# A feature pass by Strassen's seven products in two halves of tokens, its input sums made in the pass before

## The reference, cut to what matters

```python
xn = _rms_norm(x, norm_g[l]) * (1.0 + sc_x) + sh_x
fx_in, fx_gate, qx, kx, vx, nx_gate = _split_proj(xn @ w_in[l])     # 1024 channels -> 3072, 2048 tokens
qx = _rms_norm(_heads(qx), q_norm_g[l])
kx = _rms_norm(_heads(kx), k_norm_g[l])
f_out = _fourier(fx_in, w_four[l]) * jax.nn.silu(fx_gate)
na_out = _neighbourhood_attention(qx, kx, vx, kc, vc, rel_bias[l]) * jax.nn.silu(nx_gate)
```

## Time and profile before

| | |
|---|---|
| median of 3 runs | 3400.0 us (3398.42 to 3401.95) |
| the profiled execution | 3402.36 us, span 3400.6 us, mean granted clock 0.949 |
| TensorE, matmuls | busy 3111.9 us of the span |
| VectorE, ScalarE, GpSimd | busy 1514.0, 941.8, 795.5 us |
| second token pass | from 1845 to 2113 us of the span |
| second feature pass | from 2114 to 2693 us, its first products inside the token pass's last tile |
| next stage (Fourier) | its first matmul at 2699.78 us |

### The profile page before, as it was taken

One profiled execution on the slowest core, in us unless ns is written; L12 is line 12 of the kernel. 1 busy time (PEld: TensorE's weight loads), 2 busy tenths in 40 slices (PEclk: granted clock), 3 DMA queues, 4 the chain that ended last, 5 costly groups with the idle time before them and its releaser, 6 DMA issues. The chain is left out here.

```text
span 3400.6 us, 39668 instructions
## 1 busy us (share of the span) xinstructions
PE 3111.9 (92%) x14503; PEld 2445.2 (72%) x14503; DVE 1514.0 (45%) x2504; ACT 941.8 (28%) x1520; POOL 795.5 (23%) x842
## 2 busy tenths in 40 slices
PE   3799999999988999775998999899999898999899
PEld 2588887888876666553897877677888675666687
DVE  6643333042306666386455222476000145777633
ACT  4422212110112334342222234322011133555400
POOL 5322222111112222265342222011111041000111
PEclk7899999999998999778898999999999998999999
DMA  7534335122243341314102666323211235776475
GB/s 272 184 97 116 102 101 180 61 77 75 75 127 87 90 105 55 90 47 97 43 26 82 200 185 208 109 112 123 74 74 74 99 102 134 155 158 142 112 199 148
DMA packets 325559, 390.82 MB, mean 115 GB/s; under 512 B 93879, under 2 KB 260264, under 8 KB 310696
## 3 DMA queue, kind: packets, MB, share of 16 engines
q1 hardware_dynamic: 320692, 387.11, 39.9%
q10 hardware_dynamic: 4704, 1.59, 0.2%
HBM read 256.77 MB, written 135.79 MB: 115 GB/s over the span
## 5 line engine op out<-in xcount | busy, mean ns | idle before, releaser
L691 PE MATMUL f_psum_out<-f_x_high,f_w_high 128*128 128x512 f32 (+1 forms) x1472 | 573.5, 390 | 18.8 <-DVE f_x_low L668 8.1
L691 PE MATMUL f_psum_out<-f_x_low,f_w_high 128*128 128x512 f32 (+1 forms) x1472 | 569.0, 387 | 0.0
L691 PE MATMUL f_psum_out<-f_x_high,f_w_low 128*128 128x512 f32 (+1 forms) x1472 | 568.6, 386 | 0.0
L691 PEld LDWEIGHTS f_psum_out<-f_x_high,f_w_high 128*128 128x128 f32 x1472 | 279.1, 190 | 77.9 <-issue 15.0
L691 PEld LDWEIGHTS f_psum_out<-f_x_low,f_w_high 128*128 128x128 f32 x1472 | 278.9, 189 | 56.5 <-issue 1.7
L691 PEld LDWEIGHTS f_psum_out<-f_x_high,f_w_low 128*128 128x128 f32 x1472 | 278.9, 189 | 55.5
L1351 PE MATMUL nbr_psum_o<-nbr_probT,nbr_v 128*128 128x512 f32 (+3 forms) x576 | 235.8, 490 | 0.0
L683 POOL CAST f_w_high<-f_w 128x1024 fp32r<-128x1024 f32 x41 | 42.6, 1040 | 747.8 <-PE f_psum_out L691 550.5
L532 PE MATMUL p_psum_proj<-p_w_high,p_h_high 128*128 128x512 f32 x512 | 207.5, 405 | 7.4 <-issue 4.0
L532 PE MATMUL p_psum_proj<-p_w_low,p_h_high 128*128 128x512 f32 x512 | 202.1, 395 | 0.0
L532 PE MATMUL p_psum_proj<-p_w_high,p_h_low 128*128 128x512 f32 x512 | 202.1, 395 | 0.0
(11 more groups left out here) (541 smaller groups left out, 6134.0 us busy)
## 6 DMA issues: line engine op xcount, KB each, us to landing
f_w<-in_w_fm SPq DMA_DIRECT2D x45, 512.0 KB, 5.7
side_ada_w<-in_w_ada_rows SPq DMA_DIRECT2D x24, 512.0 KB, 5.7
scratch_qkmT<-p_qkT_out SPq DMA_DIRECT2D x32, 384.0 KB, 4.6
scratch_z1T<-f_out SPq DMA_DIRECT2D x10, 1024.0 KB, 4.8
p_z<-scratch_z1T SPq DMA_DIRECT2D x16, 640.0 KB, 6.6
p_xt<-in_x SPq DMA_DIRECT2D x16, 512.0 KB, 3.9
p_staging<-in_w_tok SPq DMA_DIRECT2D x8, 1024.0 KB, 8.0
scratch_hT<-p_h_slot SPq DMA_DIRECT2D x16, 512.0 KB, 3.3
```

What stands on the lines that cost most here:

```text
L691: last = nc.tensor.matmul(self.p_out[b][:, n * BANK + lo:n * BANK + hi], self.w_parts[b][w_part][:, k, :], self.x_parts[x_part][:, n, k, l ...
```

## The change

The feature pass is made of 2x2 block products. An item is a pair of output blocks (two blocks of 128 channels) by half of the tokens (1024), so there are 24 items. In an item the weights are quadrants A (block of channels x half of k) and the input quadrants B (half of k x even or odd tiles of tokens), and Strassen's scheme in Winograd's form makes the four results of seven products: each has 4 slices of k x 3 passes = 12 matmuls of 128x128 by 128x512, the moving operand being four runs of 128 columns. This is 24 x 7 x 12 = 2016 matmuls in place of 24 x 96 = 2304.

- The four weight sums of an item are made by GpSimd (`add_weights`), the seven high parts by ScalarE (`round_w`), the seven low parts by GpSimd (`rest_of_w`). Each pair's weights are loaded twice, once for each half.
- The four input sums (T1 to T4) are made once for each pair of tiles in the token pass (`combine`: GpSimd, VectorE for the last pair) and stored beside the three plain quadrants in the scratch tensor `x2q`; x0 to x6 are loaded from it, 7 MB for each half of the tokens. For the second half they are loaded while item 11 runs, each behind the product that read it last.
- The products go through four banks of PSUM in turn, and VectorE adds them up into the outputs (`merge`, 8 operations of 128x512 in an item). Sums and transposes use two other pairs of banks. The items' order alternates kinds (`F2_ORDER`): qk, v, qk, v, qk, in, qk, in, then four gates. An item's `norm` runs inside the next item, its reciprocal in pieces of 512. The pass is written out without loops.

```diff
+class QuadrantPass:
+    A11, A12, A22, S1, S2, S3, S4 = range(7)
+    B11, B21, B22, T1, T2, T3, T4 = range(7)
+    PRODUCTS = ((A11, B11), (S2, T2), (A12, B21), (S3, T3), (A22, T4), (S1, T1), (S4, B22))
+    N, HK, BANKS = 7, KB // 2, 4
...
+    def load_w(self, sp, n):
+        if n >= 2:
+            sp.wait_ge(self.a_ready, self.N * (n - 1))
+        sp.dma_start(self.w[n % 2][:].rearrange("p m k c -> p m (k c)"),
+                     self.w_dram[self.blocks[n]:self.blocks[n] + 2].rearrange("m p c -> p m c")).then_inc(self.w_in[n % 2], 16)
+    def load_x(self, sp, half, i):
+        if half:
+            sp.wait_ge(self.prod_ready, self.N * (half * self.per_half - 1) + i + 1)
+        sp.dma_start(self.x[i][0][:].rearrange("p t k c -> p (t k c)"),
+                     self.x_dram[self.PRODUCTS[i][1], :, half * 4 * BANK:(half + 1) * 4 * BANK]).then_inc(self.x_in[i], 16)
+    def round_x(self, act, half, i):
+        act.wait_ge(self.x_in[i], 16 * (half + 1))
+        self.nc.scalar.activation(self.x[i][1][:], self.x[i][0][:], ACT.Copy).then_inc(self.x_rounded, 1)
+    def rest_of_x(self, dve, half, i):
+        dve.wait_ge(self.x_rounded, self.N * half + i + 1)
+        self.nc.vector.tensor_tensor(self.x[i][2][:], self.x[i][0][:], self.x[i][1][:], ALU.subtract).then_inc(self.x_ready, 1)
...
+    def add_weights(self, pool, n):
+        nc, w = self.nc, self.w[n % 2]
+        a11, a12, a21, a22 = (w[:, m, k:k + self.HK] for m in range(2) for k in (0, self.HK))
+        s1, s2, s3, s4 = (self.sums[:, i] for i in range(4))
+        pool.wait_ge(self.w_in[n % 2], 16 * (n // 2 + 1))
+        pool.drain()
+        nc.gpsimd.tensor_tensor(s1, a21, a22, ALU.add)
+        nc.gpsimd.tensor_tensor(s3, a11, a21, ALU.subtract)
+        pool.drain()
+        nc.gpsimd.tensor_tensor(s2, s1, a11, ALU.subtract)
+        pool.drain()
+        nc.gpsimd.tensor_tensor(s4, a12, s2, ALU.subtract).then_inc(self.sums_ready, 1)
+    def round_w(self, act, n, i):
+        a = self.PRODUCTS[i][0]
+        if n:
+            act.wait_ge(self.prod_ready, self.N * (n - 1) + i + 1)
+        if a < self.S1:
+            act.wait_ge(self.w_in[n % 2], 16 * (n // 2 + 1))
+        else:
+            act.wait_ge(self.sums_ready, n + 1)
+        self.nc.scalar.activation(self.a_high[:, i], self.quadrant(n, a), ACT.Copy).then_inc(self.a_rounded, 1)
+    def rest_of_w(self, pool, n, i):
+        pool.wait_ge(self.a_rounded, self.N * n + i + 1)
+        self.nc.gpsimd.tensor_tensor(self.a_low[:, i], self.quadrant(n, self.PRODUCTS[i][0]), self.a_high[:, i], ALU.subtract)\
+            .then_inc(self.a_ready, 1)
...
+    def product(self, pe, n, i):
+        pe.wait_ge(self.a_ready, self.N * n + i + 1)
+        if n % self.per_half == 0:
+            pe.wait_ge(self.x_ready, self.N * (n // self.per_half) + i + 1)
+        if self.N * n + i >= self.BANKS:
+            pe.wait_ge(self.prod_free, self.N * n + i + 1 - self.BANKS)
+        a_parts, x_parts = (self.a_high, self.a_low), self.x[i][1:]
+        for k in range(self.HK):
+            for at, (w_part, x_part) in enumerate(PASSES):
+                last = self.nc.tensor.matmul(self.bank(n, i), a_parts[w_part][:, i, k, :], x_parts[x_part][:, :, k, :],
+                                             start=(k == 0 and at == 0), stop=(k == self.HK - 1 and at == len(PASSES) - 1))
+        last.then_inc(self.prod_ready, 1)
...
+    def combine(eng, ops, j):
+        b11, b21, b12, b22 = (slot[b][:, k:k + HK] for b in range(2) for k in (0, HK))
+        t1, t2, t3, t4 = (combined[:, n] for n in range(4))
+        eng.wait_ge(combined_stored, 16 * (j + 1))
+        ops.tensor_tensor(t1, b12, b11, ALU.subtract)
+        ops.tensor_tensor(t3, b22, b12, ALU.subtract)
+        eng.drain()
+        ops.tensor_tensor(t2, b22, t1, ALU.subtract)
+        eng.drain()
+        ops.tensor_tensor(t4, t2, b21, ALU.subtract)
+        eng.drain().then_inc(combined_ready, 1)
...
             def move(j, b):
-                i = 2 * j + b
+                i, of_pair = 2 * j + b, bass.ds(j * BANK, BANK)
+                quadrants = d["x2q"].rearrange("s p c -> p s c")
                 wait_apart(sp, x_filled, i + 1, taken)
-                sp.dma_start(cols_of(d["x2T"], i), slot[b][:]).then_inc(slot_stored[b], 16)
+                if b == 0:
+                    sp.dma_start(quadrants[:, 0:2, of_pair], slot[0][:].rearrange("p (s k) c -> p s (k c)", s=2))\
+                        .then_inc(slot_stored[0], 16)
+                else:
+                    sp.dma_start(quadrants[:, 2, of_pair], slot[1][:, HK:].rearrange("p k c -> p (k c)")).then_inc(slot_stored[1], 16)
+                    wait_apart(sp, combined_ready, j + 1, taken)
+                    sp.dma_start(quadrants[:, 3:7, of_pair], combined[:].rearrange("p s k c -> p s (k c)")).then_inc(combined_stored, 16)
...
+            def begin_next():
+                sp.wait_ge(w_ready, MB)
                 for b in range(2):
-                    fp.load(sp, d["w_fm2"], 0, b)
-            def begin_next():
+                    sp.wait_ge(slot_stored[b], 16 * (NT // 4 + 1))
+                sp.wait_ge(combined_stored, 16 * (NT // 4 + 1))
+                fp.load_w(sp, 0)
+                fp.load_x(sp, 0, 0)
+            def go_on():
+                sp.wait_ge(gated[1], PAIRS)
+                fp.load_w(sp, 1)
+                sp.wait_ge(mix_ready[1], PAIRS)
+                sp.wait_ge(o_ready, NT - 1)
+                fp.load_x(sp, 0, 1)
                 sp.wait_ge(slices_used, 1)
-                fp.load_input(sp, d["x2T"], 0, 2)
-                sp.wait_ge(x1_ready[1], PAIRS)
-                fp.load_input(sp, d["x2T"], 2, 3)
+                fp.load_x(sp, 0, 2)
+                fp.load_x(sp, 0, 3)
             for k in range(BUFFERS, MB):
                 sp.wait_ge(w_ready, k - BUFFERS + 1)
                 begun.load_w(sp, k)
-            tiles(sp, tile, next_weights, begin_next)
+            tiles(sp, tile, begin_next, go_on)
+            sp.wait_ge(slices_used, 2)
+            fp.load_x(sp, 0, 4)
+            fp.load_x(sp, 0, 5)
+            fp.load_x(sp, 0, 6)
             move(PAIRS - 1, 1)
...
                     low(j + 1, b)
+                if b == 0 and not first:
+                    wait_apart(pool, x_filled, 2 * j, taken)
+                    combine(pool, nc.gpsimd, j - 1)
             def begin_next():
-                for b in range(2):
-                    fp.rest_of_first_weights(nc, pool, b)
+                pool.wait_ge(gated[1], PAIRS)
+                fp.add_weights(pool, 0)
+                for i in range(fp.N):
+                    fp.rest_of_w(pool, 0, i)
             low(0, 0, slice(LOW_FIRST, MB))
             low(0, 1)
...
-            fp.rest_of_input(nc, dve, 2)
+            def begin_next():
+                fp.rest_of_x(dve, 0, 0)
+                fp.rest_of_x(dve, 0, 1)
+            tiles(dve, tile, before_last=begin_next)
+            fp.rest_of_x(dve, 0, 3)
+            dve.wait_ge(xT_ready, NT)
+            dve.wait_ge(slot_stored[1], 16 * PAIRS)
+            dve.wait_ge(combined_stored, 16 * PAIRS)
+            for k in range(KB):
+                nc.vector.tensor_scalar(slot[1][:, k, :], p_x[:, k, :], g.scale_x[:, k:k + 1], g.shift_x[:, k:k + 1], ALU.mult, ALU.add)
+            dve.drain().then_inc(x_filled, 1)
+            dve.wait_ge(x_filled, NT)
+            combine(dve, nc.vector, PAIRS - 1)
+            for i in range(4, fp.N):
+                fp.rest_of_x(dve, 0, i)
...
+F2_ORDER = (0, 4, 1, 5, 2, 6, 3, 7, 8, 9, 10, 11)
...
+            for n in range(LAST + 1):
+                if n + 2 <= LAST:
+                    fp.load_w(sp, n + 2)
+                if kind(n - 1) in ("qk", "v"):
+                    store(n - 1)
+                if n == fp.per_half - 1:
+                    for i in range(N):
+                        fp.load_x(sp, 1, i)
+                if kind(n) in ("in", "gate"):
+                    store(n)
...
+            def aside(n, b):
+                used = among(n, "qk", "v")
+                if used:
+                    pe.wait_ge(aux_free[b], used)
+                if kind(n) == "qk":
+                    pe.wait_ge(sq_ready[b], among(n, "qk") + 1)
+                    for c in range(0, HT, BANK):
+                        last = nc.tensor.matmul(p_aux[b][:, c:c + BANK], ones[:], work[b][:, c:c + BANK], start=True, stop=True)
+                    last.then_inc(sum_ready[b], 1)
+                elif kind(n) == "v":
+                    pe.wait_ge(out_ready[b], n + 1)
+                    for c in range(0, HT, P):
+                        last = nc.tensor.transpose(p_aux[b][:, c:c + P], out[n % 2][b][:, c:c + P], g.ident[:])
+                    last.then_inc(turned[b], 1)
...
+            def merge(n, i):
+                first, second = out[n % 2]
+                await_product(n, i)
+                if i == 0:
+                    await_row(n, 0)
```

(35 more changed lines are left out.)

351 lines of the change are left out of this document (196 added, 155 removed).

## The result

The changed kernel takes **3472.8 us**, median of 4 runs (3468.82 to 3473.71); the kernel before takes 3401.0 (3398.42 to 3403.39). The ratio is 1.0209, with an interval of 1.0191 to 1.0227.

The account below looks back on a forecast made before the run. TensorE was taken to bound the feature pass, a ring of loads and stores the token pass. 3402.4 + 40 (token pass) - 10 (feature pass) - 1 (last stores) = 3431, less 2.4 for the median: 3429 us, range 3386 to 3464.

Parts of the forecast that it names:

- The port, 6: Feature pass: norm operations lengthened by SBUF sharing with GpSimd, allowed 0.75 us a norm, about 6 us in all.
- The bound of 44 us: Feature pass: upper limit for that sharing, if every such operation and cast stood behind a whole GpSimd operation.
- Clock, 7: Feature pass: TensorE's clock drops behind four waits of over 6 us, 1.7 us lost each, 7 us.
- Token pass, +40: Token pass: SP's wait for combine delays odd tiles' loads, 38 us over pairs 1 to 6, plus 2 for the clock.
- The ring: Token pass: loads, gating, rounding, fill, store and next load set the period; an added wait lengthens it, 6.3 us a pair.
- TensorE's own work, 482.5: Feature pass: TensorE's matmuls, sums and transposes left after product 4 starts, without waits, 482.5 us.
- The norm's timeline, 27 and 12: Items behind qk items: VectorE's norms and merges hold TensorE, 27 us behind v items and 12 behind "in" items.
- Refill, 4: Loading x0 to x6 for the second half: low parts ahead of item 12's merge 0 make TensorE wait, 4 us.
- Entry, 31.5: From the token pass's last matmul to product 4: late loads, rounding, subtracting and barrier, 31.5 us.
- Port and refill are worse: Rival, feature pass: two-input operations wait more behind GpSimd's and the refill runs at half rate, 3464 us; chance 0.2.
- the token pass's wait is covered: Rival, token pass: SP's wait for combine ends before loads are needed, only the feature pass's gain is left, 3389 us; 0.1.
- VectorE keeps up: Rival, feature pass: norms fit, so their waits and slow clock go, 3377 us; 0.1 shared with both faster rivals together.

Follow-up runs that it names:

- run 2: Changed kernel with GpSimd's weight sums and low parts in the feature pass replaced by constant fills that read nothing: 3437.5 us.
- run 3: Changed kernel with each reciprocal of the norms replaced by a minimum with 0.001, so normalisation is left out: 3403.1 us.
- run 8: Kernel of run 7 with merge 0 copying into a spare buffer, so the wait for the row's store moves to merge 2: 3362.6 us.
- Run 5: Changed kernel with pair sums stored behind the odd tile's loads and stores, and x1 to x3 loaded ahead of pair 6's sums' store: 3435.8 us.
- Run 9: Kernel of run 8 with ScalarE's fills awaiting sums made, not stored, x4 and x5 loaded later, VectorE's last-tile work earlier: 3346.0 us.
- run 7: Changed kernel with sums' store, item order, entry and refill rearranged, plus second reciprocal, scaling and merge 6 reordered on VectorE: 3398.7 us.

## Why the prediction was right in direction and wrong in size

It said 3429, in 3386 to 3464; 3472.8 lies above. Both mechanisms, a token pass made longer by a wait in SP's queue and a feature pass held up by VectorE, came as told. The sizes did not. By its own steps, with what was measured over what was forecast: token pass 45.2 for 40; entry 40.3 for 31.5; TensorE's own work 486.0 for 482.5; waits in the pass 61.1 for 49 (27 + 12 + 6 + 4); slow clock 22.8 for 7.

- **The port, 6, and the clock behind it. This step failed most.** It allowed 0.75 us a norm; a norm grew by 1.39 in the mean, by 2.9 in the four that follow merge 5 in an "in" item. Of the waits of the pass, GpSimd's reads made 25.6 us (run 2), 21.1 without the refill's part, for 6; another 11.9 followed as slow clock, for which this step had nothing. The bound of 44 us given beside it held the 37. The Trainium skill (SBUF — State Buffer, Who interferes with whom) says that a VectorE instruction with two SBUF inputs shares a read interface with GpSimd instructions that read SBUF, that GpSimd instructions which only write don't meet it, and that casts can contend as well. The trace agrees on all three: the subtraction takes 1879 ns in the mean for 1226, and 1226 again beside fills; the cast takes 1.61 us for 0.69 in the four "in" items. The Trainium skill (SBUF — State Buffer, Who interferes with whom) also says that who issues first decides who blocks. The eight casts ahead of merge 5 fit that: the one at 2222.61 began 0.28 us ahead of a GpSimd subtraction and kept its 0.70 us, and the subtraction took 1.57 for 1.29.
- **Clock, 7.** It was 22.8 in the pass: 9.5 behind the four waits of 7.6 (1.4 to 2.9 each), 7.7 behind the four of 4.0, 2.6 behind the refill's and 3.0 behind the entry's. One wait cost 2.3 in the mean for the 1.7 taken, and the number of waits was wrong: ten, not four. By itself this is the largest difference in the sum, 15.8 us.
- **Token pass, +40.** The ring came as forecast: the pair shown grew by 6.2 us (forecast 6.3), and by the loads of y 39.1 us of the 45.2 lie between the fourth and the last of them, in six long steps (forecast 38). Another 2.3 lie ahead of these and 3.8 behind the last load of y, for 2 forecast. TensorE's six waits for y are 5.6 to 7.8 us. So the step was a few us too small, and the earlier start by 5.1, which is luck, hid that in the total.
- **TensorE's own work, 482.5.** 569.9 - 61.1 - 22.8 = 486.0 after, 483.6 in run 3, 486.2 in run 8. The matmuls of the products start 0.227 us apart in the median, as those of the kernel before: a product with four runs of 128 columns costs what one of 512 costs.
- **The norm's timeline, 27 and 12.** With GpSimd's reads gone (run 2) the waits were 6.2 at the transposes, for 6.8 forecast, and 1.2 + 0.8 behind "in" items, for 3.1. This base was 6.5 us too high in all and hid part of what the port's step lacked.
- **Refill, 4.** It was a wait of 7.4, and 10 with its slow clock: merge 0 stood behind four low parts, which took 12.42 us and not 9.2, again beside GpSimd (4.5 of the 7.4 went with GpSimd's reads, and are in the port's 25.6 too).
- **Entry, 31.5.** 40.3, counted as the forecast did from the end of the turn of x that follows the last matmul, 0.9 us later than in the table. The last turn of x began 22.2 us behind that point, for 14.5; the rest took 18.1, for 17. The step had only x2's and x3's loads wait for slices of the last tile's matmuls; x1's stood behind the store of pair 6's sums as well, for whose third operation GpSimd took 3.15 us beside VectorE's 2.84 us for x0:

```profile
2145.41 3.15 POOL L2182 TENSOR_TENSOR p_combined<-p_slot,p_combined 128x512 f32<-128x512 f32 x1
```
```profile
2150.14 0.39 SPq L2214 DMA_DIRECT2D scratch_x2q<-p_combined  x1
2150.58 0.51 SPq L765 DMA_DIRECT2D f_w<-in_w_fm  x1
2151.19 3.43 SPq L771 DMA_DIRECT2D f_x<-scratch_x2q  x3
```

  The last tile's sum, square and factor then followed x1, x2 and x3 in three queues. Run 5 gave 4.4 of the 8.8 back; how the rest divides among the three queues was not taken apart.
- **The rivals.** "Port and refill are worse", at 3464, came nearest, in part by luck: it gave 16 more to the port and 19 more to the refill, where the port's waits took 15 more (without the refill), the refill 3 more, and the slow clock and the entry, which it left as they were, made up the difference. That the token pass's wait is covered, or that VectorE keeps up, was false for the change as made. Run 9 has both nearly made true, with another order of items and of the entry besides, and its 3346 is near the 3337 that the two would give together.

## What to carry to other kernels

A saving on the engine that bounds a stage is kept only as far as the next engine's queue is ordered for it. Here 65 us of matmuls cost 31 us in entry and pass as written, and gained 53 there (580.6 less 33.5 and 493.8) with the same operations in another order. Place each operation by the bank that waits for it, put a wait for a store as late in the item as it can stand, and keep waits for something just made out of the queue that issues the next loads. When the elementwise work of two engines is priced, find which of the operations ahead of the meeting point run beside the other engine, add the lengthening of each, and add the slow clock behind each wait that is left.

## What was not expected of the hardware

- Either engine can be the one that pays when VectorE and GpSimd meet. VectorE's multiply took 2.35 us for 1.28, its cast 1.61 for 0.69 and its subtraction 2.14 for 1.23 beside GpSimd operations of 1.3 us; GpSimd's took 3.14 to 3.34 us for 1.29 beside VectorE subtractions that take 2.3 us alone.
- Every wait of TensorE of 4.0 us and more in the pass, the one at its start included, 43 in the eleven kernels with the change, was followed by work at 1.2 GHz, 2.7 to 6.2 us long. Of the waits of 2.6 to 3.7 us 15 of 18 were, of those of 2.0 to 2.1 us 14 of 20, and of the 28 of 1.6 us none; what decides between 2 and 4 us was not settled.
- A 1 MB store took 8.3 us from issue to landing with two 1 MB loads and a store still under way in front of it (run 7), and 5.2 us with none.
